# Reordering the attention loop of layer A: value products ahead of transposes, a projection and half of the values behind the first logits

## The reference: two decoder layers

```
q_lat, c_kv, q_idx, k_idx, w_idx = split(h @ w_in)       # 16 heads x 128 latent; one shared latent
score = sum_j w_idx[j] * relu(q_idx[j] . k_idx)          # 8 index heads
idx   = the 128 keys of highest score, among the causal ones
p     = softmax(q_lat . c_kv[idx] * R**-0.5 + rel_bias)  # per head, 128 queries x keys so far
o     = p @ c_kv[idx];  o = o @ w_uv[head];  x += o @ w_out
```

## Time and profile before

| | us |
|---|---|
| median of 3 runs | 1229.24 (1227.66 to 1229.34) |
| the profiled execution | 1229.2 |
| its span, first to last instruction | 1227.4 |
| PE busy in the span | 1174.9 (96%) |
| DVE, ACT, POOL busy | 594.4, 464.5, 581.4 |
| mean granted TensorE clock | 0.986 of full |

### The profile page before, as it was taken

The page is one execution under the profiler, slowest core; times in us unless marked ns, Lnnn a source line. Parts: engine busy times, 40 slices in busy tenths (PEclk is TensorE's granted clock), DMA queues, the critical chain, the costliest instruction groups (busy, mean ns, idle before and its releaser), DMA issues.

```text
span 1227.4 us, 16258 instructions
## 1 busy us (share of the span) xinstructions
PE 1174.9 (96%) x5600; PEld 968.2 (79%) x5600; DVE 594.4 (48%) x1031; ACT 464.5 (38%) x857; POOL 581.4 (47%) x319
## 2 busy tenths in 40 slices
PE   5999999999999999999999989899999999999996
PEld 4767888878888888888888778778888888888885
DVE  5479866654644444442222479855544444431111
ACT  4262346654333222323222467634322233322222
POOL 4344846675454444544445464215444455444441
PEclk8999999999999999999999989899999999999998
DMA  5831401113233333223332542112333323323331
GB/s 166 238 101 34 155 21 50 37 50 104 71 102 101 103 103 98 82 78 89 94 94 82 146 111 53 36 31 81 96 103 103 95 82 96 92 73 94 92 94 69
DMA packets 178468, 110.42 MB, mean 90 GB/s; under 512 B 7180, under 2 KB 173127, under 8 KB 178424
## 3 DMA queue, kind: packets, MB, share of 16 engines
q1 hardware_dynamic: 177984, 108.69, 31.1%
q10 hardware_dynamic: 440, 1.17, 0.3%
HBM read 107.70 MB, written 6.33 MB: 93 GB/s over the span
## 4 chain that ended last, share of the span: by engine, by line
PE 79%; DVE 8%; POOL 5%; issue 3%; DMA 2%; ACT 2%; SPq 0%; DVEq 0%; ACTq 0%; POOLq 0%
PE ps L547 25%; PE ps L549 25%; PE ps L548 25%; POOL prob L495 2%; POOL w_lo L440 2%; PE ps L753 1%; DMA b_toep<-bias_toep 1%; DVE work L1420 1%; DMA x_tok<-in_x 1%; DVE b_prob L1658 1%; DVE ss L1362 1%; PE ps L556 1%; DVE xs_lo L1349 1%; DVE work L1404 1%; DVE bpt_lo L1305 1%
## 5 line engine op out<-in xcount | busy, mean ns | idle before, releaser
L440 POOL TENSOR_TENSOR w_lo<-raw,w_hi 128x1024 fp32r<-128x1024 f32 (+1 forms) x200 | 463.0, 2336 | 509.4 <-ACT w_hi L967 500.3
L547 PE MATMUL ps<-xs_hi,w_hi 128*128 128x512 f32 (+3 forms) x1024 | 400.4, 391 | 7.9 <-DVE x L1345 3.6
L549 PE MATMUL ps<-xs_hi,w_lo 128*128 128x512 f32 (+3 forms) x1024 | 395.2, 386 | 0.0
L548 PE MATMUL ps<-xs_lo,w_hi 128*128 128x512 f32 (+3 forms) x1024 | 395.1, 386 | 0.0
L967 ACT CAST w_hi<-raw 128x1024 fp32r<-128x1024 f32 (+1 forms) x196 | 178.9, 962 | 432.9 <-PE ps L549 418.5
L547 PEld LDWEIGHTS ps<-xs_hi,w_hi 128*128 128x128 f32 x1024 | 192.8, 188 | 52.2 <-DVE x L1345 3.8
L548 PEld LDWEIGHTS ps<-xs_lo,w_hi 128*128 128x128 f32 x1024 | 192.9, 188 | 38.7 <-issue 1.1
L549 PEld LDWEIGHTS ps<-xs_hi,w_lo 128*128 128x128 f32 x1024 | 192.8, 188 | 38.7
L547 PE MATMUL ps<-act_hi,w_hi 128*128 128x512 f32 x352 | 139.2, 396 | 0.0
L549 PE MATMUL ps<-act_hi,w_lo 128*128 128x512 f32 x352 | 138.0, 392 | 0.0
L548 PE MATMUL ps<-act_lo,w_hi 128*128 128x512 f32 x352 | 136.6, 388 | 0.0
(11 more groups left out here) (186 smaller groups left out, 1402.5 us busy)
## 6 DMA issues: line engine op xcount, KB each, us to landing
raw<-in_ffn_w_gate_up SPq DMA_DIRECT2D x88, 512.0 KB, 4.7
raw<-in_ffn_w_down SPq DMA_DIRECT2D x32, 384.0 KB, 3.6
raw<-in_a_w_in SPq DMA_DIRECT2D x21, 512.0 KB, 4.8
raw<-in_ffn_w_down SPq DMA_DIRECT2D x32, 320.0 KB, 4.0
raw<-in_b_w_in SPq DMA_DIRECT2D x10, 512.0 KB, 5.0
bias_toep<-bias_row SPq DMA_DIRECT2D x1, 4096.0 KB, 21.9
toep<-bias_toep SPq DMA_DIRECT2D x16, 256.0 KB, 2.6
raw<-in_a_w_out SPq DMA_DIRECT2D x8, 512.0 KB, 4.5
```

What stands on the lines that cost most here:

```text
L440: nc.gpsimd.tensor_tensor(pieces(w_lo, n)[half], pieces(raw, n)[half], pieces(w_hi, n)[half].bitcast(F32), ALU.subtract)\
L547: nc.tensor.matmul(dst, wh, xh, start=start, stop=False, **kw)
L548: nc.tensor.matmul(dst, wh, xl, start=False, stop=False, **kw)
L549: return nc.tensor.matmul(dst, wl, xh, start=False, stop=stop, **kw)
```

## The change

On PE, `weigh(k-3)` is put ahead of `turn(k-2)` in each iteration. On ACT and DVE the order follows: `heads_hi` and `heads_lo` are put ahead of `turned_hi` and `turned_lo`, and so ahead of `exponents(k)` and `lowest(k)`. The first two iterations are written out anew. On PE: `values(0..3)`, `logits(0)`, `logits(1)`, the projection of head 15 (`q_tile(3, 2)`, which stood ahead of all of these), `values(4..7)`. ACT, DVE and POOL follow with the cast, the scaling and the low part of head 15; on DVE `invert(0)` now stands behind `lowest(1)`, and on POOL `normalise(0)` stands ahead of the low part of head 15. No instruction, semaphore or DMA is added or taken away; SP's queue is the same.

```diff
--- before.py
+++ after.py
@@ -483,7 +483,7 @@
                     pool.wait_ge(uvh_done, 1)
                     nc.gpsimd.tensor_tensor(uv_lo[:, :, :], uv_raw[:, :, :], uv_hi[:, :, :].bitcast(F32),
                                             ALU.subtract).then_inc(uvl_done, 1)
-            for h in range(13, H):
+            for h in range(13, H - 1):
                 q_part(h)
 
             def normalise(h):
@@ -494,7 +494,9 @@
                     at = prob[par][:, OFF[i]:OFF[i] + (i + 1) * P]
                     nc.gpsimd.tensor_scalar(at, at, rinv[:, par, i:i + 1], None, ALU.mult).then_inc(nrm_done, 1)
 
-            for k in range(1, H + 1):
+            normalise(0)
+            q_part(H - 1)
+            for k in range(2, H + 1):
                 normalise(k - 1)
                 if k in (13, 14):
                     split_lo_half(S_AO, k - 13)
@@ -674,7 +676,7 @@
             with pe.Fori(0, 2) as i:
                 for v in range(4):
                     q_tile(v, i)
-            for v in range(4):
+            for v in range(3):
                 q_tile(v, 2)
 
             def out_first(s0, hi, lo, done, ks, per=1):
@@ -768,16 +770,20 @@
                                pt_hi[:, h % 2, c0:c0 + n], pt_lo[:, h % 2, c0:c0 + n], s == 0, s == NB - 1)
                 last.then_inc(o_done, 1)
 
-            for k in range(H + 3):
-                if 2 <= k < H + 2:
-                    turn(k - 2)
+            for j in range(4):
+                values(j)
+            logits(0)
+            logits(1)
+            q_tile(3, 2)
+            for j in range(4, 8):
+                values(j)
+            for k in range(2, H + 3):
                 if k >= 3:
                     weigh(k - 3)
+                if k < H + 2:
+                    turn(k - 2)
                 if k < H:
                     logits(k)
-                if k < 2:
-                    for j in range(4 * k, 4 * k + 4):
-                        values(j)
                 if k == H:
 
                     pe.wait_ge(neg_done, 4 * H)
@@ -1112,16 +1118,20 @@
                 act.wait_ge(o_done, h + 1)
                 nc.scalar.copy(oT_hi[own(h), h // 2, :], ps[own(h), 6 + h % 2, :]).then_inc(oTh_done, 1)
 
-            for k in range(H + 3):
-                if 2 <= k < H + 2:
+            for j in range(4):
+                value_hi(j)
+            exponents(0)
+            exponents(1)
+            q_head(H - 1)
+            for j in range(4, 8):
+                value_hi(j)
+            for k in range(2, H + 3):
+                if k >= 3:
+                    heads_hi(k - 3)
+                if k < H + 2:
                     turned_hi(k - 2)
                 if k < H:
                     exponents(k)
-                if k >= 3:
-                    heads_hi(k - 3)
-                if k < 2:
-                    for j in range(4 * k, 4 * k + 4):
-                        value_hi(j)
                 if k in (12, 13):
                     split_late(S_AO, k - 12, 8)
             for half in range(2):
@@ -1449,7 +1459,6 @@
                 n = (i + 1) * P
                 nc.vector.tensor_scalar(mask[:, OFF[i] - P:OFF[i] - P + n], work[:, OFF[i] - P:OFF[i] - P + n],
                                         TAKEN / 2, BIG, ALU.is_ge, ALU.mult).then_inc(mask_done, 1)
-            q_scale(15, 3, 1)
 
             def lowest(k):
                 par = k % 2
@@ -1493,18 +1502,23 @@
                 dve.wait_ge(exp_done, 4 * h + 4)
                 nc.vector.reciprocal(rinv[:, h % 2, :], rsum[:, h % 2, :]).then_inc(rinv_done, 1)
 
-            for k in range(H + 3):
-                if 1 <= k <= H:
+            for j in range(4):
+                value_lo(j)
+            lowest(0)
+            lowest(1)
+            invert(0)
+            q_scale(H - 1, 3, 1)
+            for j in range(4, 8):
+                value_lo(j)
+            for k in range(2, H + 3):
+                if k <= H:
                     invert(k - 1)
-                if 2 <= k < H + 2:
+                if k >= 3:
+                    heads_lo(k - 3)
+                if k < H + 2:
                     turned_lo(k - 2)
                 if k < H:
                     lowest(k)
-                if k >= 3:
-                    heads_lo(k - 3)
-                if k < 2:
-                    for j in range(4 * k, 4 * k + 4):
-                        value_lo(j)
 
             def out_proj(u0, e, bias):
                 with dve.Fori(0, 2) as i:
```

## The result

The changed kernel takes 1217.89 us, the median of 4 runs (1216.88, 1217.07, 1218.71, 1218.91). The kernel before took 1229.29 beside it (1227.66 to 1231.41, 4 runs). The ratio is 0.9906, with a 95% interval from 0.9888 to 0.9925: faster by 11.4 us. The forecast was 1218.1.

A forecast was written before the change was run, and what follows sets the result against it. PE's products bound most of the kernel; in attention A's loop PE waited for POOL. Head 15's logits ending 10.0 us earlier plus 1.16 at the end gave 11.1 us, from 1229.2 to 1218.1, range 1215.5 to 1222.5.

The forecast's parts named there:

- C: Rival, loop: value product heading PE's queue waits for the whole DVE and ACT order; slower, 1242 us; chance 0.03.
- D: Rival, loop: POOL stays the bound at 12.56 us for two heads; 1228 us; chance 0.03.
- A: Rival, start: the clock still falls before the first transposes; gain 9.4 us, 1219.8 us; chance 0.20.
- B: Rival, loop: DVE and ACT's ring is longer than its parts, 5.95 us per head, 1224.0 us; chance 0.10.
- the cast and the low part of the value product: Loop, ACT and DVE: 0.62 and 0.69 us stand before the row-sum inversion only by DVE's order, delaying POOL.
- Per head 5.50: Changed loop: 5.50 us per head, bounds 5.45 (PE alone) and 5.70; 71.5 us for 13 heads, before 80.65.
- the ring: Loop: cycle of DVE and ACT steps, 5.32 us per head (5.25 with overlapping latencies), 0.13 below PE's 5.45.
- The start: Before the loop: first transposes come 0.51 us earlier, the hole shrinks to 1.78 us; head 1's logits 3.0 us earlier.
- The clock: Behind the hole before the first transposes: full clock returns, gaining all 1.71 us; bounds all or none.
- The half slabs: Loop, two heads: ACT's casts of output weights cost 1.4 us in all, bounds 0 and 2.1.
- POOL's spare of 0.8: Loop: POOL's multiplications end 0.8 us before transposes want them, so POOL's wait goes; just covers the half slabs.
- The end: From head 15's logits to the output projection: 2.95 us instead of 4.11, gain 1.16.

The follow-up runs named there:

- e2: Kernel before with only ACT's and DVE's loop order changed; PE's order and the start stay old: 1230.3 us, ratio 1.0007.
- e1: Kernel before with only PE's loop order changed (value product ahead of transposes); ACT, DVE and the start stay old: 1220.44 us, ratio 0.9933.
- e8: Changed kernel plus one DVE memset per head in iterations 3 to 15, between the value product's and the transposes' low parts: 1224.07 us, ratio 0.9956 to kernel before.
- e5: Changed kernel with ACT's two casts of output-weight half slabs moved ahead of the exponentials of heads 12 and 13: 1218.55 us, ratio 0.9908 to kernel before.
- e9: Changed kernel plus two POOL memsets ahead of the multiplications of heads 2 to 11: 1218.27 us, ratio 0.9912 to kernel before.
- e3: Kernel before with the new loop order on PE, ACT and DVE, but the old start: 1219.94 us, ratio 0.9927.
- e0: The changed kernel again, unaltered, as base for later runs: 1218.35 us, ratio 0.9912 to the kernel before.
- e4: Changed kernel's new start with the old loop order on PE, ACT and DVE: 1228.23 us, ratio 0.9988 to the kernel before.
- e6: Changed kernel where the first transposes wait for six values' low parts, not eight; the first value product waits for all: 1217.28 us, ratio 0.9907 to kernel before.
- e7: Changed kernel with the edits of e5 and e6, plus head 15's query cast on ACT behind value casts 4 and 5: 1215.30 us, ratio 0.9888 to kernel before.
- e10: e7 with half-slab casts in iterations 11 and 13, POOL's low parts in 12 and 14: 1215.42 us, ratio 0.9882 to the kernel before.

## Why the prediction was right, and where it was not

**The sum.** Forecast 11.1 us, 11.75 in the stage, 11.4 between the medians. The range and the sign held. Of the rivals, C and D did not come; A's loss of clock came in another place, and of B only a small part.

**What bounds the loop: right in the engine, wrong in the cause.** The prediction said that the cast and the low part of the value product "stand in front of the inversion only by DVE's order", and so took their 0.62 and 0.69 us, and POOL's wait, for a matter of that order. This is the step that failed. e2 makes just that change of order and gains nothing. e1 leaves it out and gains 9 us. What held the loop was the value product on PE. In the old order PE's queue had transposes, value product and logits, so the chain of two heads ran from POOL's multiplications of head h over its transposes, *then 1.94 us of value product*, then the logits of head h + 2 and so on to the multiplications of that head. The chain of waits of the kernel before, which the earlier trace rows shows in part, has these pieces between its two uses of POOL (start, us, what):

```profile
212.62 0.55 PE ps L753 x3
213.20 0.66 PE ps L753 x4
218.26 0.69 DVE prob L1466
```

Between the second and the third lie the value product, from 213.61 on, and the logits, from 215.56 on. With the value product taken out, 12.56 - 1.94 = 10.6 us are left for two heads, less than the 10.9 that PE needs for them; and PE becomes the bound, as e1's 5.42 per head shows. The number came out right because the forecast of the loop had also priced the right cause, the 1.94 us of other work between logits and transposes, and because PE's own time per head, which then decides, was read well.

**Per head 5.50 was too much by 0.07.** Measured 5.43: PE alone, 13 x 0.07 = 0.9 us more gain. That is below the 5.45 to 5.55 that the prediction named as its sign. It had 5.45 for PE and added 0.05 for hand-overs in the ring. The Trainium skill (Perfetto Trace Analysis, Optimizing Scalar/DVE Operations), whose rule of overlapping latencies would have had PE alone decide, fits the time. But the ring of 5.25 us that comes with that rule is not borne out here: by e8 the ring is near 5.35, which is closer to the 5.32 that the prediction took from the rows. Rival B, which let the ring be longer than the sum of its rows, was right by some 0.03 us and wrong in the size it needed. The margin that I took for 0.13 us is about 0.08.

**The start.** Gain 0.43 against 0.51; the hole is 1.68 us by the profile where 1.78 was said. The term holds. One reading beside it is wrong: the logits of head 1 come not 3.0 but 5.4 us earlier (163.42 against 168.86 by the prediction's own figures; in the traces 5.25 us behind the stage's start in place of 10.63). No term rests on it.

**The clock.** What the clock took behind the first transposes' hole comes back, as forecast: from these transposes to the end of head 2's logits 3.59 us pass (177.53 to 181.12) where it was 5.22, a gain of 1.63 for a forecast of 1.71. The evidence for it, that a hole that ended at 120.00 cost nothing, was poor: in the profiled execution of the change just that hole cost 1.6 us (last section). A single execution's clock row was read as a property of the hole, and that the term came right was in part luck.

**The half slabs.** Forecast 1.4 us; the two heads take 0.52 and 1.05 us more than 5.43, 1.57 in all. That POOL's 6.66 us per head would be "just" covered by its spare and ACT's delay held in the change, where PE doesn't wait for POOL; e5 shows how narrowly, as with ACT's delay gone the end becomes 1.2 us longer. POOL's spare of 0.8 was a lower bound; e9 finds 1.1 without a wait.

**The end.** 1.20 against 1.16. The term needs ACT's and DVE's order too: with PE's alone (e1) the end stays at 4.00 us. No part of the gain was given back later.

**What it would have looked like, had it been wrong.** The prediction asked for no wait for POOL before the transposes, waits before value products in two heads only, clock 1.00 behind the first transposes, and the output projection at 255.3. The first three are in the rows above. The projection is at 256.19, which is 254.72 once the later start of 1.47 is taken off.

## What to carry to other kernels

Where several engines with their own queues pass heads to one another, write down the dependent chain over as many iterations as it spans, here from one use of POOL to the next but one, and ask which instruction lies in it only because it is next in some engine's queue. Move that one, on the engine on which it delays the others; moving its followers within the chain (e2) gained nothing here. Then look at the second chain before adding work: here it was within 0.1 us of the first, while POOL, the old bound, had over a microsecond per head to give away. And look behind the loop: what an edit gains inside it (e5) can be lost again at its end.

## What the runs showed of the hardware

The clock behind a hole of PE. Here is PE's row at the hole that all kernels of this study share, in the trace of the change:

```profile
119.85 0.50 PE L549 MATMUL ps<-xs_hi,w_hi 128*128 128x512 f32 x1 [2.19 <-POOL w_lo L440]
```

Over the thirteen profiled executions, the granted clock afterwards fell to 0.50 (1.2 of 2.4 GHz) or did not:

| hole before | clock 0.50 behind it |
|---|---|
| 2.29 us, first transposes (before, e1, e2, e3) | 4 of 4 |
| 2.15 to 2.19 us, at 120 (all thirteen) | 7 of 13 |
| 1.68 us, first transposes (after, e0, e4, e5, e8, e9) | 0 of 6 |
| 0.49 us or none, first transposes (e6, e7, e10) | 0 of 3 |

Where it falls at 120, the stage starts 39.8 to 39.9 us behind the end of the hole, elsewhere 38.2 to 38.3: 1.6 us, with the same instructions in this stretch. The hole's length doesn't tell which: 2.15 and 2.17 us occur on both sides. I had not expected one and the same hole to cost nothing in one execution and 1.6 us in the next. Whether that is also why the first four runs of the change lie in two pairs 1.7 us apart is an inference: e0's runs don't repeat it, and the mean granted clock of the four runs (0.987 and 0.989 in the slower pair, 0.988 and 0.991 in the faster) doesn't decide it. What in the hole or in the work around it decides was not tried; the holes before the first transposes differ in the work around them as well as in length.

A second surprise is smaller. The memset of e8 is 0.48 us in its row, with the next instruction starting 0.41 after it, but it lengthened the sequence on DVE by 0.54 in one head and 0.66 in the next. In the first the row ahead of it also lost what it had saved by running into its successor (0.74 to the next start in place of 0.61).
